# The back half of a decoder layer rebuilt: full-sequence merge, output projection by token chunk, mix and u2 in SBUF, one weight ring for the feed-forward part

## The chip, the cores and the metric

The kernel runs on the 8 cores of one Trainium2 chip. Each core computes one sequence of the batch by itself; the cores do not talk to each other. The time of a run is the device time of the slowest core in microseconds (us). A core has TensorE (PE, the matmuls), VectorE (DVE), ScalarE (ACT), GpSimd (POOL) and SyncE (SP); the last three can also issue DMAs.

## The reference, cut to what matters

```python
# x: (8, 2048, 2048) float32, one decoder layer
u    = rms_norm(x, norm_mix_pre)
proj = u @ w_in                      # q,k,v of 2 x 8 heads of 128, forget logits, g_sb, g_fx
o_sb, o_fx = stick_breaking(...), forgetting_attention(...)        # each (2048, 1024)
merged = sigmoid(g_sb) * (o_sb @ w_branch_sb) + sigmoid(g_fx) * (o_fx @ w_branch_fox)
mix  = merged @ w_out
h    = x + rms_norm(mix, norm_mix_post)
u2   = rms_norm(h, norm_ffn_pre)
ff   = (silu(u2 @ w_gate) * (u2 @ w_up)) @ w_down                  # inner width 5632
out  = h + rms_norm(ff, norm_ffn_post)
```

## The kernel before, in words

Everything is held transposed: model width on the 128 partitions in KC = 16 blocks, tokens along the free axis. A matmul is 128x128 weights by 128x512 tokens; NCH = 4 chunks of 512 tokens make the sequence of 2048, FC = 44 blocks the feed-forward width. The order on each engine is the order in which the program is written out; `kb.op`, `kb.group` and `kb.dma` put semaphore waits in front of an instruction for the last writer and the readers of each buffer (`Res`), and an engine or DMA queue runs its list strictly in that order. `Filler.tick` hands out items of side work while a main loop is written.

The front half (first norm, 16 attention heads with the projections as filler, and the gates `gts`, which go to DRAM as do the head outputs `OTs`) ends with the last piece of the last head: its weights are transposed by DMA into `WTB`, PE multiplies them with V (`pv`), DVE copies the result and SP stores it.

The back half works on halves of 1024 tokens (`TH`), `hf` = 0 and 1:

- `P5(hf)` (merge): one 4 MB load of the head outputs (`OTh`), then for each of 16 blocks the branch weights `wb` (POOL queue), the gates `gb` (SP queue), 2 x 16 matmuls, two DVE products and a POOL sum into `merged`.
- `WOUT(hf)`: output projection, weights `wst` loaded in f32 and cast by DVE; ACT copies each result to `mixst`, stores it to DRAM (`mixs`) and squares it; PE adds up the squares with a matmul by ones (`stat_mm`) and `rstd_from_banks` makes 1/rms.
- `hpass_items`: loads x and `mixs` again, h = x + norm(mix), stored to DRAM (`hs`) by the POOL queue, squared, summed. For half 0 it is filler in `WOUT(1)`, for half 1 in `GATEUP(0)`.
- `u2_items`: loads `hs` again and writes u2. For half 0 it stands alone between `WOUT(1)` and `GATEUP(0)`, for half 1 it is filler in `DOWN(0)`.
- `GATEUP(hf)`: 44 blocks, two weight tiles of 512 KB each (three buffer pairs `wgu`), 64 matmuls; ACT takes silu, DVE the product into `aT`.
- `DOWN(hf)`: 16 blocks, one weight tile `wd` of 1408 KB (three buffers), 2 x 44 matmuls; results go to DRAM (`ffs`), squares to `stat_mm`. `DOWN(1)` runs all 16 blocks for its first 512 tokens and then all again for the other 512, so it loads every `wd` twice.
- `final_items`: loads `hs` and `ffs`, out = h + norm(ff). For half 0 filler in `GATEUP(1)`, then inside `DOWN(1)` and behind it.

`al.release` gives the SBUF of one stage to the next, so the first weights of a stage wait until the buffers that lay there are done with.

## Time and profile before

| | |
|---|---|
| median of 3 runs | 4203.94 us (4196.98 to 4696.29) |
| profiled execution | 4189.77 us |
| its span on the slowest core (core 4) | 4188.2 us |
| spans of the 8 cores | 4130.2 to 4188.2 us |
| DMA, whole span | 553.39 MB, HBM read 617.09 MB, written 109.05 MB |

The span is from the first to the last instruction of a core. Windows of the trace are given in us from the span's start. PEclk is TensorE's granted clock as a share of full speed. A matmul record is longer than the distance to the next one, since matmuls overlap; the rate is read from the busy time of a stretch divided by its matmuls.

### The profile page before, as it was taken

Reading aid. Unit: us, or ns where it says so; the run is one execution under the profiler, and the core shown is the slowest. Engines: PE = TensorE matmul, PEld = TensorE weight load, DVE = VectorE, ACT = ScalarE, POOL = GpSimd, SP = SyncE. Lnnn points to the kernel's source line nnn. Section 1 sums busy time; section 2 is a strip of 40 time slices with the busy share of each in tenths; the row PEclk is TensorE's granted clock in tenths of the full one; section 3 lists DMA queues with packets and bytes.
Section 4 is the critical chain, followed back from the end, with each engine's and each line's share of the span. In section 5 each row is a group of like instructions: output and inputs, shape, how many; then the busy total and the mean of one; then the engine's idle time right before and its main releaser. Section 6 shows DMA issues by size and latency. Waiting matters only on the chain.

```text
span 4188.2 us, 52026 instructions; the slowest of 8 cores (4130.2 to 4188.2 us)
## 1 busy us (share of the span) xinstructions
PE 3764.6 (90%) x17500; PEld 1699.2 (41%) x17500; DVE 1191.8 (28%) x1501; ACT 1046.4 (25%) x1673; POOL 737.3 (18%) x1046
## 2 busy tenths in 40 slices
PE   5999999999999969977639999989999999999973
PEld 2444444444444424433214444434444444444431
DVE  3444445656566523122131111111001111110001
ACT  3456554444444410301211111111110000001100
POOL 0111112222222213033321111110001111110113
PEclk8999999999999989989869999999999999999987
DMA  7212235666665668598885655548537666659997
GB/s 198 44 35 49 50 57 113 119 111 117 116 121 102 136 162 226 172 227 213 226 216 106 123 114 119 115 94 164 126 71 130 115 125 113 126 98 169 184 180 206
DMA packets 358390, 553.39 MB, mean 132 GB/s; under 512 B 200048, under 2 KB 208624, under 8 KB 347888
## 3 DMA queue, kind: packets, MB, share of 16 engines
q0 software_dynamic: 58768, 253.82, 33.4%
q1 hardware_dynamic: 280928, 262.68, 26.7%
q10 hardware_dynamic: 18432, 33.56, 2.5%
q8 instruction: 145, 2.38, 0.2%
q14 instruction: 117, 0.96, 0.1%
HBM read 617.09 MB, written 109.05 MB: 173 GB/s over the span
## 4 chain that ended last, share of the span: by engine, by line
PE 78%; DMA 15%; DVE 2%; issue 2%; POOL 2%; ACT 1%; SPq 0%; DVEq 0%; ACTq 0%; POOLq 0%
PE ps L83 78%; DMA fl_185_227<-ffs 3%; DMA hs<-hst_109_151 3%; DMA xs_21_63<-xT 1%; DMA wd_175_217<-wfd_t 1%; POOL hst_109_151 L83 1%; DMA WTA_95<-wp_62_104 1%; DVE uT_48 L83 1%; DMA mh_107_149<-mixs 1%; DMA hl_133_175<-hs 1%; DMA OTh_136<-OTs 1%; DMA OTh_115<-OTs 1%; DMA WTA_95<-wp_61_103 1%; DMA wd_177_219<-wfd_t 0%; DMA mh_106_148<-mixs 0%
## 5 line engine op out<-in xcount | busy, mean ns | idle before, releaser
L83 DVE TENSOR_TENSOR_SCAN Pr_59_101<-kap_55_97 128x640 f32<-128x640 f32 (+4 forms) x96 | 160.1, 1667 | 124.1 <-POOL kap_55_97 L83 123.3
L83 PE MATMUL ps<-u_124_166,wgu_0_143_185 128*128 128x512 bf16 x480 | 111.1, 385 | 56.3 <-DVE u_124_166 L83 56.3
L83 PE MATMUL ps<-uT_48,wgt_64_106 128*128 128x512 bf16 x704 | 160.5, 379 | 0.0
L83 PE MATMUL ps<-uT_48,wgt_65_107 128*128 128x512 bf16 x704 | 160.0, 379 | 0.0
L83 PE MATMUL ps<-uT_48,wbf_1_8_50 128*128 128x512 bf16 x512 | 128.1, 399 | 34.0 <-DVE uT_48 L83 23.1
L83 PE MATMUL ps<-uT_48,wgt_66_108 128*128 128x512 bf16 x640 | 145.6, 379 | 0.0
L83 PE MATMUL ps<-aT_167,wd_175_217 128*128 128x512 bf16 x484 | 116.3, 404 | 19.9 <-DMA wd_175_217<-wfd_t 19.9
L83 DVE TENSOR_TENSOR_SCAN Pr_60_102<-kap_56_98,Pr_60_102 128x512 f32<-128x512 f32 (+3 forms) x64 | 116.3, 1818 | 48.3 <-ACT kap_56_98 L83 43.6
L83 PE MATMUL ps<-aT_167,wd_153_195 128*128 128x512 bf16 x528 | 117.0, 382 | 13.3 <-DMA wd_153_195<-wfd_t 13.3
L83 POOL TENSOR_SCALAR_AFFINE_SELECT kap_55_97<-kap_55_97 128x128 f32<-128x128 f32 x96 | 40.0, 416 | 485.5 <-ACT kap_55_97 L83 485.1
L83 PE MATMUL ps<-uT_48,wbf_0_7_49 128*128 128x512 bf16 x512 | 121.4, 385 | 0.0
L83 PE MATMUL ps<-uT_48,wbf_1_11_53 128*128 128x512 bf16 x512 | 121.3, 383 | 0.0
L83 PE MATMUL ps<-uT_48,wbf_2_12_54 128*128 128x512 bf16 x512 | 119.6, 379 | 0.0
L83 PE MATMUL ps<-uT_48,wbf_2_9_51 128*128 128x512 bf16 x512 | 119.3, 379 | 0.0
L83 PE MATMUL ps<-uT_48,wbf_0_10_52 128*128 128x512 bf16 x512 | 119.0, 379 | 0.0
L83 PE MATMUL ps<-u_124_166,wgu_0_167_209 128*128 128x512 bf16 x480 | 109.9, 382 | 9.9 <-DMA wgu_0_167_209<-wfg_t 9.9
L83 PE MATMUL ps<-aT_167,wd_176_218 128*128 128x512 bf16 x484 | 107.7, 382 | 6.8 <-DMA wd_176_218<-wfd_t 6.8
L83 PE MATMUL ps<-aT_167,wd_177_219 128*128 128x512 bf16 x440 | 100.9, 391 | 12.8 <-DMA wd_177_219<-wfd_t 12.7
L83 PE MATMUL ps<-u_124_166,wgu_1_170_212 128*128 128x512 bf16 x480 | 108.5, 379 | 0.0
L83 PE MATMUL ps<-u_124_166,wgu_1_168_210 128*128 128x512 bf16 x480 | 108.5, 379 | 0.0
L83 PE MATMUL ps<-u_124_166,wgu_0_169_211 128*128 128x512 bf16 x480 | 108.5, 379 | 0.0
L83 PE MATMUL ps<-u_124_166,wgu_1_144_186 128*128 128x512 bf16 x480 | 108.5, 379 | 0.0
(429 smaller groups left out, 6253.0 us busy)
## 6 DMA issues: line engine op xcount, KB each, us to landing
wd_175_217<-wfd_t POOLq DMA_DIRECT2D x11, 1408.0 KB, 19.0
wd_176_218<-wfd_t POOLq DMA_DIRECT2D x11, 1408.0 KB, 18.5
wd_177_219<-wfd_t POOLq DMA_DIRECT2D x10, 1408.0 KB, 19.8
gts<-gst_67_109 SPq DMA_DIRECT2D x43, 256.0 KB, 2.7
gts<-gst_68_110 SPq DMA_DIRECT2D x43, 256.0 KB, 2.8
gts<-gst_69_111 SPq DMA_DIRECT2D x42, 256.0 KB, 2.9
wd_153_195<-wfd_t POOLq DMA_DIRECT2D x6, 1408.0 KB, 11.6
xs_21_63<-xT SPq DMA_DIRECT2D x8, 1024.0 KB, 16.5
```

The costliest lines, as they stand in the source:

```text
L83: ins = getattr(eng, meth)(**kw)
```

## The change

The front half keeps its instructions; a few buffers move, `OTs`, `gts`, `hs` and `ffs` get a layout in which one load is one contiguous piece of DRAM, and `mixs` is gone. In the back half:

- Merge: all four token chunks of a block follow each other, so each `wb` tile is loaded once. `hook0` to `hook3` start its first loads inside the last head, and merge groups are written between the end of the last head and its last `pv`. DVE makes the sum too.
- Output projection by token chunk, with all 16 weight tiles `wo` in SBUF. `mix` stays in SBUF (20 tiles); `h_item` makes h for the chunk before, stores it, squares it and writes h times the gain over the merge result `M` in bf16. The factor 1/rms of u2 is left out there and is multiplied in `GATEUP` (`rstd2`), in two more DVE instructions for each block and chunk.
- `ring`: the 8 tiles `wo0` to `wo7` become one ring for all feed-forward weights in their order of use; `wd` comes in three pieces of 16, 16 and 12 blocks. A step's tiles are refilled when the step is done.
- The order of `DOWN(1)`: 11 blocks run for both chunks, 5 (9 to 13) for the first chunk only, in between; these 5 follow at the end for the second chunk. Results stay in SBUF (`ff`). `final1` finishes the first chunk during the last 5 blocks and loads `hs` of the second chunk into the buffers it has just stored from.

Names: SP in a DMA row is the queue that issues it; `OT_70`, `OT_71`, `OT_83`, `OT_84` are the head outputs of token chunks 0 to 3, `G_..` the gates, `hm_..` and `ff_0_..` in the last rows are `hl1` and `ff[c][0]`.

PE at the end of the last head, before (`kT`, `qT` scores and `wgt` gates are the last head's, `WTB` its `pv`, `OTh` the merge):

```order
L83 MATMUL ps<-kT_35_77,qT_34_76 128x512 x2
L83 MATMUL ps<-uT_48,wgt_65_107 128x512 x24
L83 MATMUL ps<-WTB_96,V_36_78 128x512 x13
L83 MATMUL ps<-WTB_96,V_36_78 128x384
L83 MATMUL ps<-WTB_96,V_36_78 128x256
L83 MATMUL ps<-WTB_96,V_36_78 128x128
L83 MATMUL ps<-OTh_115,wb_74_116 128x512 x32
```

The same place in the changed kernel:

```order
L83 MATMUL ps<-uT_48,wgt_65_107 128x512 x24
L83 MATMUL ps<-OT_70_112,wb_72_114 128x512 x16
L83 MATMUL ps<-OT_71_113,wb_72_114 128x512 x16
L83 MATMUL ps<-OT_70_112,wb_75_117 128x512 x16
L83 MATMUL ps<-WTB_96,V_36_78 128x512 x13
L83 MATMUL ps<-WTB_96,V_36_78 128x384
L83 MATMUL ps<-WTB_96,V_36_78 128x256
L83 MATMUL ps<-WTB_96,V_36_78 128x128
L83 MATMUL ps<-OT_71_113,wb_75_117 128x512 x16
L83 MATMUL ps<-OT_83_125,wb_72_114 128x512 x16
L83 MATMUL ps<-OT_83_125,wb_75_117 128x512 x16
L83 MATMUL ps<-OT_84_126,wb_72_114 128x512 x16
```

Three merge groups now stand ahead of the last `pv`, and one between it and the first group that reads chunk 2.

SP at the same place before, with the semaphores that each issue waits for (`d_..` are DMAs, `d_Ost1` the store one row above; `e_dve` and so on are engines):

```order
L83 DMA_TRANSPOSE WTB_96<-wp_63_105 128x8x128 [waits e_dve_3]
L83 DMA OTs<-Ost_17_59 128x512 [waits e_dve_3]
L83 DMA OTh_115<-OTs 128x16x1024 [waits d_Ost0_17,d_Ost1_18,e_pe_1,d_v0_0_20,d_v0_1_21,d_v0_2_22,d_v0_3_23,d_v1_0_33,d_v1_1_34,d_v1_2_35,d_v1_3_36]
L83 DMA gb_77_119<-gts 128x1024 [waits e_act_2,e_pool_4]
L83 DMA gb_77_119<-gts 128x1024
```

SP at this place in the changed kernel:

```order
L83 DMA_TRANSPOSE WTB_96<-wp_63_105 128x8x128 [waits e_dve_3]
L83 DMA G_73_115<-gts 128x1024 [waits e_dve_3]
L83 DMA G_74_116<-gts 128x1024 [waits d_gst1_44,e_dve_3]
L83 DMA G_77_119<-gts 128x1024 [waits e_dve_3]
L83 DMA OTs<-Ost_19_61 128x512 [waits e_dve_3]
L83 DMA OT_83_125<-OTs 128x8192 [waits d_Ost0_21,e_pool_4,e_act_2]
L83 DMA OT_84_126<-OTs 128x8192 [waits d_Ost1_22,d_wp0_37,d_wp1_38,d_wp2_39,e_pe_1,d_wgt0_40,d_xs1_0_27,d_xs1_1_28,d_xs1_2_29,d_xs1_3_30]
L83 DMA G_78_120<-gts 128x1024 [waits d_gst2_45,e_dve_3]
```

The one load of a half has become loads of single chunks: those of chunks 2 and 3 stand behind the last store of the head, those of chunks 0 and 1 have moved into the head.

SP in the last blocks, before:

```order
L83 DMA hl_0_189_231<-hs 128x512 [waits d_hl2_0_122,e_pool_4]
L83 DMA fl_192_234<-ffs 128x512 [waits d_ffst0_114,d_fl0_125,e_dve_3]
L83 DMA hl_1_190_232<-hs 128x512 [waits d_hl2_1_123,e_pool_4]
L83 DMA fl_193_235<-ffs 128x512 [waits d_ffst1_115,d_fl1_126,e_dve_3]
L83 DMA hl_2_191_233<-hs 128x512 [waits d_hl2_2_124,e_pool_4]
```

SP in the last blocks of the changed kernel (`d_ff0_0` is the store of `ff_0_204`, two rows above the wait, `d_ff9_0` that of `ff_0_222`):

```order
L83 DMA outT<-ff_0_204_246 128x512 [waits e_dve_3]
L83 DMA hm_236_278<-hs 128x512 [waits d_hb0_76,d_hm0_123]
L83 DMA ff_0_204_246<-hs 128x512 [waits d_hb0_76,d_ff0_0_91]
L83 DMA outT<-ff_0_222_264 128x512 [waits e_dve_3]
L83 DMA hm_237_279<-hs 128x512 [waits d_hm1_124]
L83 DMA ff_0_222_264<-hs 128x512 [waits d_hb1_77,d_ff9_0_109]
```

The stores have moved from the POOL queue into this one, and each load into an `ff` buffer waits for the store two rows above it; there are 16 such triples, and behind them the 16 stores of the second chunk.

The core of the diff:

```diff
+    def hook0():
...
+        ot_load(0)
+        wb_load(0)
+        g_load()
+        g_load()
+
+    def hook1():
+        ot_load(1)
...
+    def hook3():
+        ot_load(2)
+        ot_load(3)
+
+    def m_group():
...
+        for j in range(2):
+            bt, br_ = banks[pr_[j]]
+            kb.op(DVE, "tensor_tensor", dict(out=g.t[:, j, :], in0=bt[:, :], in1=g.t[:, j, :], op=ALU.mult),
+                  writes=[br_], part=[g.r])
+        kb.op(DVE, "tensor_tensor", dict(out=M[tc].t[:, c, :], in0=g.t[:, 0, :], in1=g.t[:, 1, :], op=ALU.add),
+              reads=[g.r], part=[M[tc].r])
+        g_load()
...
+    while mcnt["g"] < len(m_order):
+        m_group()
+        if mcnt["g"] % 8 == 0 and mcnt["g"] >= 24:
+            wo_load(nwo)
+            nwo += 1
...
+    def h_item(tc, c):
...
+        kb.op(DVE, "scalar_tensor_tensor", dict(out=h_.t[:, :], in0=mx.t[:, :], scalar=gcol(1, c),
+                                                in1=rm.t[:, :], op0=ALU.mult, op1=ALU.mult),
+              reads=[mx.r, gains.r, rm.r], writes=[h_.r])
+        kb.op(DVE, "tensor_tensor", dict(out=h_.t[:, :], in0=h_.t[:, :], in1=x_.t[:, :], op=ALU.add),
+              reads=[x_.r], writes=[h_.r])
+        x_fetch()
+        kb.dma(SP, h_.ds, hs[c, tc], h_.t[:, :], reads=[h_.r], writes=[h_res[c][tc]])
+        kb.op(ACT, "activation", dict(out=q_.t[:, :], in_=h_.t[:, :], func=AF.Square), reads=[h_.r], writes=[q_.r])
+        kb.op(DVE, "tensor_scalar", dict(out=M[tc].t[:, c, :], in0=h_.t[:, :], scalar1=gcol(2, c), scalar2=None,
+                                         op0=ALU.mult), reads=[h_.r, gains.r], part=[M[tc].r])
...
+    def ring_fill():
+        while rc_["i"] < min(len(rq), rc_["u"] + 8):
+            src, nf = rq[rc_["i"]]
+            sl = ring[rc_["i"] % 8]
+            kb.dma(POOL, sl.ds, sl.t[:, 0:nf, :], src, writes=[sl.r])
+            rc_["i"] += 1
...
+                kb.op(DVE, "tensor_tensor", dict(out=tb.t[:, :], in0=bg[:, :], in1=r2.t[:, :], op=ALU.mult),
+                      reads=[r2.r], writes=[rg, tb.r])
+                kb.op(ACT, "activation", dict(out=tb.t[:, :], in_=tb.t[:, :], func=AF.Silu), writes=[tb.r])
+                kb.op(DVE, "tensor_tensor", dict(out=tb.t[:, :], in0=tb.t[:, :], in1=r2.t[:, :], op=ALU.mult),
+                      reads=[r2.r], writes=[tb.r])
+                kb.op(DVE, "tensor_tensor", dict(out=aT[f].t[:, t, :], in0=bu[:, :], in1=tb.t[:, :], op=ALU.mult),
+                      reads=[tb.r], writes=[ru], part=[aTr[t]])
...
+    def final1(k):
+        c = fin_order[0][k]
+        final_mul(c, 0)
+        final_add(c, 0)
+        if k + 4 < KC:
+            h_fetch1(fin_order[0][k + 4], 0)
+        c1 = fin_order[1][k]
+        hl_ = ff[c][0]
+        kb.dma(SP, hl_.ds, hl_.t[:, :], hs[c1, 3], reads=[h_res[c1][3]], writes=[hl_.r])
+        h1[(c1, 1)] = hl_
```

## Rows read from the trace of the kernel before

**Rows 1.** The page, part 1: busy us, share of the span, instructions

```profile
PE 3764.6 (90%) x17500; PEld 1699.2 (41%) x17500; DVE 1191.8 (28%) x1501; ACT 1046.4 (25%) x1673; POOL 737.3 (18%) x1046
```

**Rows 2.** Windows of core 4: length, busy per engine, PEclk, DMA share, GB/s

```profile
1533.00:1656.00 123.00, 113.42 (x512) 50.04 (x512) 42.72 (x65) 0.00 (x0) 47.05 (x45) 0.97 0.88 206
...
1776.00:1803.00 27.00, 1.24 (x4) 0.43 (x5) 1.31 (x2) 4.61 (x7) 1.62 (x3) 0.57 0.96 250
1803.00:1917.00 114.00, 112.12 (x511) 50.23 (x509) 43.07 (x64) 0.00 (x0) 46.55 (x45) 0.98 0.87 203
1917.00:2145.00 228.00, 149.01 (x576) 60.55 (x576) 45.15 (x52) 60.90 (x104) 70.94 (x66) 0.86 0.86 229
2145.00:2194.00 49.00, 0.00 (x0) 0.00 (x0) 24.05 (x32) 0.20 (x1) 2.64 (x5) 0.50 0.85 196
2194.00:2812.00 618.00, 617.47 (x2848) 279.20 (x2848) 81.78 (x120) 73.79 (x121) 102.09 (x146) 1.00 0.56 112
2812.00:2825.00 13.00, 0.17 (x1) 0.14 (x2) 2.98 (x5) 3.80 (x5) 1.60 (x3) 0.57 0.87 144
...
3137.00:3149.00 12.00, 0.52 (x2) 0.23 (x3) 1.35 (x2) 3.39 (x6) 3.17 (x6) 0.69 0.85 155
3149.00:3764.00 615.00, 609.20 (x2816) 275.64 (x2814) 81.95 (x120) 53.82 (x89) 103.66 (x149) 1.00 0.63 117
3764.00:3935.00 171.00, 163.00 (x725) 71.97 (x726) 0.69 (x1) 19.11 (x33) 8.44 (x16) 0.96 0.99 171
3935.00:4133.00 198.00, 165.98 (x716) 71.70 (x714) 13.65 (x18) 22.90 (x37) 36.68 (x45) 0.93 0.94 192
4133.00:4189.00 56.00, 0.00 (x0) 0.00 (x0) 12.36 (x16) 0.00 (x0) 29.42 (x32) 0.50 0.70 197
```

**Rows 3.** Timeline at the end of the last head: start, us, what, idle before

```profile
1485.05 5.34 PE L83 MATMUL ps<-uT_48,wgt_65_107 128*128 128x512 bf16 x24
...
1499.08 5.25 PE L83 MATMUL ps<-WTB_96,V_36_78 128*128 128x512 bf16 x16 [8.68 <-DMA WTB_96<-wp_63_105]
...
1506.90 0.37 SPq L83 DMA_DIRECT2D OTh_115<-OTs  x1
1507.42 14.22 SPq L83 DMA_DIRECT2D gb_77_119<-gts  x2
```

**Rows 4.** DMA issues: count, KB each, median us from issue to landing

```profile
gts<-gst_67_109 SPq DMA_DIRECT2D x43, 256.0 KB, 2.7
...
OTh_115<-OTs SPq DMA_DIRECT2D x1, 4096.0 KB, 25.8
...
gb_98_140<-gts SPq DMA_DIRECT2D x16, 512.0 KB, 7.5
...
wgu_0_167_209<-wfg_t POOLq DMA_DIRECT2D x15, 512.0 KB, 8.3
...
fl_164_206<-ffs SPq DMA_DIRECT2D x16, 256.0 KB, 6.2
...
ffs<-ffst_178_220 ACTq DMA_DIRECT2D x16, 256.0 KB, 13.9
...
outT<-ot_195_237 POOLq DMA_DIRECT2D x6, 256.0 KB, 6.2
```

**Rows 5.** Instructions by shape: count, busy us, mean ns, idle before

```profile
L83 DVE TENSOR_TENSOR aT_167<-ps,sg_149_191 128x512 bf16<-128x512 f32 x44 | 30.4, 692 | 264.0 <-PE ps L83 252.8 <-issue 11.2
...
L83 DVE SCALAR_TENSOR_TENSOR hst_138_180<-mh_136_178,gains_45,rstdm_113 128x512 f32<-128x512 f32 x16 | 11.9, 743 | 0.0
...
L83 ACT ACTIVATE mixst_88_130<-ps 128x512 f32<-128x512 f32 x16 | 9.6, 597 | 199.0 <-PE ps L83 199.0
```

**Rows 6.** Timeline behind the last matmul

```profile
4129.73 0.38 PE L83 MATMUL ps<-sqf_181_223,cbf_43 128*128 128x512 bf16 x1 [1.72 <-ACT sqf_181_223 L83]
...
4132.46 0.75 DVE L83 SCALAR_TENSOR_TENSOR ot_195_237<-fl_192_234,gains_45,rstd_126_168 128x512 f32<-128x512 f32 x1 [1.55 <-ACT rstd_126_168 L83]
```

More of the change, by code:

```diff
@@ L369, in _emit @@
     make_qkv(0)
+    Ost = [Slot(kb, f"Ost{i}", [128, 512], BF16, dma=True) for i in range(2)]
     m_q1 = al.mark()
@@ new lines, in evict0, with fin_ready, first @@
+    def evict0(c, t, bt, br_):
+        fs = ffst[evn["n"] % 4]
+        evn["n"] += 1
+        kb.op(ACT, "activation", dict(out=fs.t[:, :], in_=bt[:, :], func=AF.Copy), writes=[br_, fs.r])
+        kb.dma(SP, fs.ds, ffs[c, t], fs.t[:, :], reads=[fs.r], writes=[ff_res[c][t]])
+    evn = {"n": 0}
+    def fin_ready(hf, t):
+        if hf == 0:
+            if t == 1:
+                def first():
+                    for _ in range(3):
+                        f_fetch()
+                hq.append(first)
+                hq.extend([lambda n=n: final0(n) for n in range(2 * KC)])
+        else:
+            hq.extend([lambda k=k: final1(k) for k in range(KC)] if t == 0 else [])
```

723 lines of the change are left out of this document (362 added, 361 removed).

## The prediction, made before the changed kernel had run

> **What bounds the kernel now.** I read the page first: PE is busy for 3764.6 of 4188.2 us, with 17,500 matmuls [rows 1]. The order of both programs has the same 17,498 matmuls, so the change can only take away time in which PE stands, and the question is where it stands. The windows by stage answer that [rows 2]. In 2194 to 2812 PE does 2848 matmuls in 617.47 us at a granted clock of 1.00, the upper level of 2.4 GHz: 0.2168 us each, with no gap. I take that as the price of a matmul. The last gate matmuls end at 1485.05 + 5.34 = 1490.4 [rows 3]; from there to the end lie 2697.8 us. In them stand the last pv (16 matmuls, 3.5 us) and 10,688 more: merge 1024, output projection 1024, gate and up 5632, down 2816, sums of squares 192. They are worth 2317.2 us. So PE stands for 377 us behind 1490.4, and the change touches no time ahead of that.
>
> The windows say where: 39 us from the last gate matmul to the first merge matmul at 1533 (42.6 less pv), 12 in the rest of the first merge (123 less 512 matmuls), 26 at the second merge's start, 103 in the second output projection with its h pass (228 less 576 matmuls), 49 while u2 is made alone, 13 and 12 at the borders of the feed-forward stages, 5 in the second gate and up, 57 in the last down stage (369 less 1441 matmuls), 55 behind the last matmul [rows 2, 3]. That is 371 of the 377.
>
> **The change part by part.**
>
> *End of the last head.* PE stood 8.7 us for the last transposes, and pv then ran for 5.25 us, cold, where 3.5 is the price [rows 3]. Three merge groups (10.4 us) now fill that gap; they need chunks 0 and 1, asked for some tens of us earlier. Then one group (3.5 us) covers what follows pv: copy (0.7 us), store, load of chunk 2. The 4096 KB load took 25.8 us [rows 4]; half of it is 12.9. Issued 1.4 us behind pv it lands at 14.3, so PE waits 10.8; two groups follow (6.9, and 1.8 for the lower clock after a gap, as pv showed), and chunk 3 lands some 4 us after them. I take 16 us; from 3 (rows of 16 KB run much faster than the 2 KB pieces before) to 25 (both loads and the gates share the DMA engines). The Trainium skill (DMA: Bandwidth & Descriptors, Anatomy of one DMA) gives 2 us and bytes over 436 GB/s for a DMA of GpSimd's queue; for 4096 KB that would be an estimated 11.6 us, and the trace's 25.8 us on SP's queue disagrees; by it a chunk would land in 6.8 us, this term would be about 5, and the time 11 us less.
>
> SP's loads inside the head stand ahead of its transposes. A 4096 KB load held up SP's next issues for 14.22 us [rows 3], so two of 2048 KB may hold it for 7 each. pv comes long behind the transposes and the three `wp` buffers give some slack; I take 3 us, 0 to 10.
>
> *Merge.* Four groups (13.9 us) ask for one `wb` and four gate tiles of 512 KB; before it was two and four, and 1803 to 1917 was 112.12 of 114 us busy at a DMA share of 0.87 [rows 2]. The gates are asked for four groups ahead, 11 us net of DVE, and landed in 7.5 [rows 4]. DVE has three products of 0.69 us [rows 5] in each 3.5. Nothing is added; the 12 and 26 us are gone.
>
> *Output projection.* Six of 16 weight tiles are loaded in the merge, ten at its end. A tile costs the 16 DMA engines at most 618 x 0.56 / 88 = 3.9 us [rows 2], with all else that ran then, so the last lands 39 + 8 us later and is used at 15 x 3.7 = 55. A block and chunk takes 18 matmuls, 3.9 us; ACT has a copy and two squares, 3 x 0.60 = 1.8, DVE three operations, at most 2.2 [rows 5]. The h pass no longer waits for `mixs` and `hs` to land, it reads SBUF, and its x loads and h stores have three buffers, 11 us. So the 103 us go. The 49 us of u2 go too: chunks 0 and 1 have been written long before gate and up starts.
>
> *Gate and up.* Per block and chunk (32 matmuls, 6.94 us) DVE has three products and for some steps three operations of side work, at most 2.1 + 2.2 us, and ACT one silu. The chain behind the gate matmuls is about 3.5 us, and PE has three bank pairs. One weight tile is used per 6.94 us, six are under way (41 us) and they land in 8.3 [rows 4]. Nothing on the path. In the second half, though, the final items now go one per step for 33 steps, 768 KB in 6.94 us. Behind the last matmul 48 such transfers of 256 KB took 56 us at a share of 0.70 [rows 2], 0.82 us each of the whole DMA; with the weights that makes 2.5 + 3.9 = 6.4 of 6.94. It fits, barely. I take 5 us, as now; 0 to 100.
>
> *Borders.* The ring loads the next stage's tiles while the last blocks run: 13 and 12 us go. What hides them is PE's own work: a stage begins with eight tiles loaded.
>
> *Last down stage.* Weights come 21 times instead of 32. Under a DMA share of 0.99 and 0.94 a load of 1408 KB took 369 / 32 = 11.5 us [rows 2]. The 16 first steps (11 of 19.1 us, 5 of 9.5) leave room. The last five take 9.5 us each; the ring holds 2.7 steps ahead, so 3.3 x 11.5 = 38 us of loads have to land in 38. They just do, alone; but the first chunk's stores and the `hs` loads go on beside them, some 22 of 0.82 us. I take 12 us of waiting, 0 to 25, for the 57 now.
>
> *Behind the last matmul.* Here lies a new wait. SP takes 16 triples: store, load, load into the buffer just stored, and the third waits for the first to land, with all later stores and loads queued behind it. A store of 256 KB landed in 2.7 us beside attention, 6.2 at the end, 13.9 under full DMA [rows 4]; with two issues a link is 3.7 us when quiet, and I take 7.8 beside the last weights. The chain starts when the first chunk's sum is known, five steps (47 + 12 us) before PE ends: 7 links are done then, 9 x 3.7 = 33 us remain, then 16 stores of the second chunk, 16 x 0.82 = 13, and 4 to land the last. Tail 50 us, against 55 now. Low: the chain keeps up, 2.7 us to 1/rms [rows 6], 16 x (0.74 + 0.69) = 23 on DVE, 6.2 to land: 32. High: links of 14.7 first, then 7: 100.
>
> *Sum.* 1490.4 + 3.5 + 2317.2 = 3811.1. Waits 16 + 3 + 5 + 12 = 36. Tail 50. Span 3897; the profiled execution lies 1.6 us above its span, 3899, and the median of the runs shown 14.2 above the profiled execution: **3913 us**, 291 less, a ratio of 0.931.
>
> **The rivals.**
>
> *The end drags.* The chain of stores runs at 14.7 us beside the weights and 7 behind them, and the last five steps wait 25: 3913 + 50 + 13 = 3976. For it: stores landed in 13.9 us in this very stage, and everything at the end is on SP. Against: the writes of `ffs` are gone and a third of the weights.
>
> *Nothing is left.* The 16, 12 and 18 of the tail go to their low ends: 3913 - 13 - 12 - 18 = 3870.
>
> *Side work crowds the second gate and up.* DVE is in order, so a final item that waits for its load holds back the products and PE's banks. 33 steps at 3 us more: 4012. For it: 6.4 of 6.94. Against: loads are asked for two steps ahead, 13.9 us, and landed in 6.2 [rows 4].
>
> *The resident weights are not resident in time.* If the ten late tiles land one after the other at 8.3 us each [rows 4], the last comes at 83, 28 us late: 3941. It needs that no two loads overlap; six did in gate and up.
>
> *Slower: the ring starves.* All feed-forward weights now pass one ring and one queue in strict order. Should a tile arrive less often than once in 6.94 us, PE runs at the tiles' pace, 176 times. The gain is used up at 6.94 + 291 / 176 = 8.6 us per tile; at 10 us the time is 3913 + 176 x 3.06 = 4452. For it: a single load already lands in 8.3 us, and DVE, GpSimd and DMA all get denser here. Against: even in the saturated last stage 1408 KB took 11.5 us, 4.2 per 512 KB, half of what would be needed.
>
> **How the numbers follow.** The forecast's own case has 0.72, the dragging end 0.12, nothing left 0.05, crowding 0.05, late resident weights 0.03, the starving ring 0.03. The range from 3870 to 3990 takes in the first three and the late weights, with the bounds of the tail, of the last steps and of chunk 2 and 3; crowding and starving stay out. About 2% is what a measurement here can tell from no change, 4120 to 4288. All cases but the last lie below it: faster 0.95, same 0.02, slower 0.03.
>
> **What would show it right or wrong.** Right: matmuls of merge chunk 0 ahead of the last pv; one gap of 10 to 15 us behind it; no gap from there to the last five blocks; a matmul at 0.217 us through all of gate and up; the chain of waits ending in stores of `ff` on SP's queue with links of 4 to 8 us. Wrong: PE waiting for `wo` tiles inside the stages (the ring), for DVE in the second gate and up (crowding), for ACT in the output projection, or a last head that takes longer than before. The forecast would also fail if PE's denser work were granted less than 1.00 of its clock, which no row here shows.

## The result, and the profile after

The changed kernel took 3917.8 us in the median of four runs (3914.6 to 3945.4), the kernel before 4203.9 beside it (4197.0 to 4217.9): a ratio of 0.932, 95% interval 0.927 to 0.938. Executions in which a die was granted a lower clock, and one of 4696.3 us of the kernel before, are left out of all times here and below. Forecast were 3913 us and 0.931. The time was right; some terms of the sum were not, and their errors cancelled. Below it is told which.

Busy times of the changed kernel, page, part 1. PE has the same 17,500 matmuls as in [rows 1], 11.5 us less busy, in a span 244 us shorter; DVE has 318 us more.

```profile
PE 3753.1 (95%) x17500; PEld 1700.1 (43%) x17500; DVE 1509.4 (38%) x2013; ACT 1053.0 (27%) x1675; POOL 443.9 (11%) x789
```

The profiled execution is the longest of the four, and for a reason ahead of the change: core 4 was granted 0.91 of its clock from 900 to 1200 and did 1279 matmuls there; before it was 1.00 and 1389. So I measure from a reference point, the last head's scores of 256 columns (the matmul that waits 1.20 us for `bet_58`), at 1373.45 on core 4 before and at 1400.68 after. From it to the end the sum of the forecast has 3897 - 1373.4 = 2523.6 us. The changed kernel took 2524.7, 2525.8 and 2520.9 on cores 0 to 2, 2543.2 on core 4, and 2521 to 2551 on all eight, 2535 in their mean.

Windows of core 0 (columns as in [rows 2], to which they answer): end of the last head, merge, output projection, gate and up, down, gate and up, down, behind the last matmul. They are cut at the first matmul of each stage but for one: 2014.95 lies behind the last sum of squares of the output projection, and gate and up had begun at 2011.09. The table below is cut there.

```profile
1376.66:1512.84 136.18, 119.23 (x544) 54.32 (x556) 64.44 (x60) 49.70 (x75) 26.62 (x40) 0.95 0.72 167
1512.84:1750.17 237.33, 225.76 (x1021) 102.13 (x1040) 132.80 (x191) 2.54 (x3) 15.33 (x29) 0.99 0.80 212
1750.17:2014.95 264.78, 253.76 (x1130) 113.79 (x1154) 98.53 (x155) 110.94 (x189) 4.24 (x8) 0.98 0.43 122
2014.95:2622.55 607.60, 604.60 (x2760) 275.44 (x2816) 212.55 (x313) 71.81 (x111) 45.90 (x87) 1.00 0.48 87
2622.55:2933.15 310.60, 309.13 (x1413) 140.84 (x1440) 0.69 (x1) 37.02 (x62) 24.38 (x46) 1.00 0.49 100
2933.15:3542.70 609.55, 605.16 (x2762) 275.63 (x2818) 226.51 (x329) 61.55 (x96) 47.49 (x90) 1.00 0.59 119
3542.70:3855.12 312.42, 309.58 (x1412) 140.77 (x1439) 16.31 (x25) 40.64 (x67) 29.71 (x56) 1.00 0.55 108
3855.12:3901.40 46.28, 0.00 (x0) 0.00 (x0) 27.76 (x44) 1.26 (x2) 0.00 (x0) 0.51 0.66 226
```

Read the PEld counts, since matmul records are missing on this core: 1440 weight loads in a down stage of 310.60 us, 0.2157 us each, at a clock of 1.00 and without a gap. Side by side with the sum of the forecast, stage by stage:

| from the reference point, us | forecast | core 0 | other cores |
|---|---|---|---|
| end of the last head | 117 + 3 = 120 | 136.2 | 130.4 to 144.2 |
| merge with the last `pv` | 3.5 + 222 + 16 = 241.5 | 237.3 | 234.8 to 241.8 |
| output projection | 246.3 | 260.9 | 258.6 to 269.9 |
| gate and up, first | 614.0 | 611.5 | 611.5 |
| down, first | 312.2 | 310.6 | 310.6 |
| gate and up, second | 610.5 + 5 = 615.5 | 609.6 | 609.5 |
| down, second | 312.2 + 12 = 324.2 | 312.4 | 312.4 to 312.8 |
| behind the last matmul | 50 | 46.3 | 46.8 to 59.4 |
| sum | 2523.7 | 2524.7 | 2520.9 to 2550.6 |

Three readings follow from it. The feed-forward part, 1844 us, has no gap but 1.3 us ahead of its last matmul. The last head, whose instructions the change leaves alone but for loads put into it, got 13 to 27 us longer. And the end of the kernel is as long as before.

**The last head.** PE at that place, core 4 (timeline; [rows 3] answers to it). The first three rows are waits that the kernel before did not have; then the three merge groups ahead of `pv`, `pv` itself without a wait (8.68 us before), one group behind it and one gap (the last row shows 12 of its 16 matmuls).

```profile
1444.38 7.34 PE L83 MATMUL ps<-uT_48,wgt_66_108 128*128 128x512 bf16 x24 [11.79 <-ACT gst_69_111 L83]
...
1478.27 5.30 PE L83 MATMUL ps<-uT_48,wgt_65_107 128*128 128x512 bf16 x16 [4.48 <-ACT gst_67_109 L83]
1487.27 0.80 PE L83 MATMUL ps<-kT_35_77,qT_34_76 128*128 128x512 bf16 x2 [3.70 <-ACT bet_58_100 L83]
...
1551.12 3.62 PE L83 MATMUL ps<-OT_70_112,wb_75_117 128*128 128x512 bf16 x16
1554.57 3.30 PE L83 MATMUL ps<-WTB_96,V_36_78 128*128 128x512 bf16 x16
1557.71 3.62 PE L83 MATMUL ps<-OT_71_113,wb_75_117 128*128 128x512 bf16 x16
1570.28 4.94 PE L83 MATMUL ps<-OT_83_125,wb_72_114 128*128 128x512 bf16 x12 [8.96 <-DMA OT_83_125<-OTs]
```

The first wait is for `gst_69`, a buffer that ACT fills with gates and SP stores. SP's queue shows why it was not free (timeline of core 4, SP alone): the load of chunk 0, two gate tiles, then the gate store, so behind 3 MB of loads. Behind the store comes a transpose whose issue alone takes 10.65 us, and the store of the third buffer, `gst_68`, has to wait for that.

```profile
1424.45 0.32 SPq L83 DMA_DIRECT2D OT_70_112<-OTs  x1
1424.94 0.33 SPq L83 DMA_DIRECT2D G_73_115<-gts  x1
1425.36 0.38 SPq L83 DMA_DIRECT2D G_74_116<-gts  x1
1425.84 1.73 SPq L83 DMA_DIRECT2D gts<-gst_69_111  x1
1427.66 0.42 SPq L83 DMA_DIRECT2D gts<-gst_67_109  x1
1428.17 10.65 SPq L83 DMA_TRANSPOSE WTB_96<-wp_63_105  x1
1438.92 0.52 SPq L83 DMA_DIRECT2D gts<-gst_68_110  x1
```

The chain of waits has the other end (start, us, what): that store landed 17.71 us after its issue, where such stores took 2.7 before [rows 4]; then ACT evicts into the buffer, and PE goes on.

```profile
1425.84 17.71 DMA gts<-gst_69_111
...
1443.63 0.61 ACT gst_69_111 L83
```

The DMA issues of the last 105 us of the head (issue to landing, us) say that the loads themselves are quick: a chunk of 2048 KB landed in 11.8 and 9.9 us, where 4096 KB took 25.8 [rows 4].

```profile
OT_70_112<-OTs SPq DMA_DIRECT2D x1, 2048.0 KB, 11.8
OT_71_113<-OTs SPq DMA_DIRECT2D x1, 2048.0 KB, 9.9
```

**The end.** Timeline of core 4 from the last matmul on ([rows 6] answers to it). PE is done at 3892.7. The 1/rms of the second chunk needs only its bank, but its first step, the `TENSOR_SCALAR` into `tmpD`, stands 24.7 us later, behind the additions of the first chunk on DVE.

```profile
3892.35 0.38 PE L83 MATMUL ps<-sqf_185_227,cbf_43 128*128 128x512 bf16 x1 [1.31 <-ACT sqf_185_227 L83]
...
3916.81 0.69 DVE L83 TENSOR_TENSOR ff_0_234_276<-ff_0_234_276,hm_239_281 128x512 f32<-128x512 f32 x1 [3.82 <-DMA hm_239_281<-hs]
3917.42 0.68 DVE L83 TENSOR_SCALAR tmpD_229<-ps 128x512 f32<-128x512 f32 x1
```

Those additions wait for loads which SP issues in its chain. Four links of it, from the chain of waits of core 4: 11.87 and 12.06 us beside the last weights, then 3.55, and 3.19 to 3.36 from there on.

```profile
3855.93 11.87 DMA outT<-ff_0_222_264
...
3868.28 12.06 DMA outT<-ff_0_206_248
...
3880.82 3.55 DMA outT<-ff_0_208_250
...
3884.86 3.19 DMA outT<-ff_0_224_266
```

### The profile page after: what moved, and what is told of

The parts are those of the page before. It is cut to its first block, busy times and chain, and to the rows that moved or that the text cites. A ratio compares the mean times of both kernels' runs of the same rounds, so it can differ in the third digit from the quotient of the medians.

```text
span 3943.9 us, 50744 instructions; the slowest of 8 cores (3879.0 to 3943.9 us)
## 1 busy us (share of the span) xinstructions
PE 3753.1 (95%) x17500; PEld 1700.1 (43%) x17500; DVE 1509.4 (38%) x2013; ACT 1053.0 (27%) x1675; POOL 443.9 (11%) x789
## 4 chain that ended last, share of the span: by engine, by line
PE 88%; DMA 6%; DVE 2%; ACT 2%; issue 1%; SPq 0%; POOL 0%; DVEq 0%; ACTq 0%; POOLq 0%
PE ps L83 88%; DMA xs_20_62<-xT 1%; DMA WTA_95<-wp_62_104 1%; DMA G_77_119<-gts 1%; DVE uT_48 L83 1%; DMA gts<-gst_69_111 0%; DMA gts<-gst_68_110 0%; DMA WTA_95<-wp_61_103 0%; SPq L83 0%; DMA outT<-ff_0_206_248 0%; ACT kap_56_98 L83 0%; DMA outT<-ff_0_222_264 0%; ACT bet_58_100 L83 0%; DMA OT_83_125<-OTs 0%; DMA hs<-hb_126_168 0%
## 5 line engine op out<-in xcount | busy, mean ns | idle before, releaser
L83 PE MATMUL ps<-uT_48,wgt_65_107 128*128 128x512 bf16 x704 | 168.8, 394 | 4.5 <-ACT gst_67_109 L83 4.5
L83 PE MATMUL ps<-uT_48,wgt_64_106 128*128 128x512 bf16 x704 | 166.7, 389 | 0.0
L83 PE MATMUL ps<-uT_48,wgt_66_108 128*128 128x512 bf16 x640 | 152.4, 392 | 11.8 <-ACT gst_69_111 L83 11.8
L83 PE MATMUL ps<-uT_48,wbf_1_8_50 128*128 128x512 bf16 x512 | 130.4, 405 | 32.7 <-DVE uT_48 L83 23.1
L83 ACT ACTIVATE tg_139_181<-tg_139_181 128x512 f32<-128x512 f32 x60 | 37.8, 630 | 338.6 <-DVE tg_139_181 L83 338.6
L83 ACT ACTIVATE tg_141_183<-tg_141_183 128x512 f32<-128x512 f32 x58 | 36.5, 630 | 334.1 <-DVE tg_141_183 L83 334.1
L83 ACT ACTIVATE tg_140_182<-tg_140_182 128x512 f32<-128x512 f32 x58 | 36.5, 629 | 330.8 <-DVE tg_140_182 L83 330.8
L83 PE MATMUL ps<-uT_48,wbf_0_7_49 128*128 128x512 bf16 x512 | 122.8, 388 | 0.0
L83 PE MATMUL ps<-uT_48,wbf_1_11_53 128*128 128x512 bf16 x512 | 122.8, 386 | 0.0
L83 PE MATMUL ps<-uT_48,wbf_2_12_54 128*128 128x512 bf16 x512 | 121.5, 383 | 0.0
L83 PE MATMUL ps<-uT_48,wbf_2_9_51 128*128 128x512 bf16 x512 | 121.0, 383 | 0.0
L83 PE MATMUL ps<-uT_48,wbf_0_10_52 128*128 128x512 bf16 x512 | 120.5, 383 | 0.0
L83 PEld LDWEIGHTS ps<-uT_48,wgt_65_107 128*128 128x128 bf16 x704 | 70.8, 101 | 92.4 <-issue 22.8
L83 PEld LDWEIGHTS ps<-uT_48,wgt_64_106 128*128 128x128 bf16 x704 | 69.8, 100 | 84.7 <-issue 19.1
L83 PEld LDWEIGHTS ps<-uT_48,wgt_66_108 128*128 128x128 bf16 x640 | 63.9, 100 | 90.5 <-issue 29.5
L83 POOL TENSOR_SCALAR_AFFINE_SELECT bet_57_99<-bet_57_99 128x128 f32<-128x128 f32 x96 | 95.7, 997 | 57.9 <-ACT bet_57_99 L83 57.7
L83 POOL TENSOR_SCALAR_AFFINE_SELECT kap_55_97<-kap_55_97 128x128 f32<-128x128 f32 x96 | 39.3, 409 | 518.0 <-ACT kap_55_97 L83 517.7
L83 PEld LDWEIGHTS ps<-uT_48,wbf_1_8_50 128*128 128x128 bf16 x512 | 52.1, 103 | 98.9 <-issue 53.3
L83 ACT ACTIVATE bet_57_99<-ps 128x640 f32<-128x640 f32 (+4 forms) x96 | 74.4, 775 | 19.3 <-ACT kap_55_97 L83 15.1
```

Source lines behind the costliest of these rows:

```text
L83: ins = getattr(eng, meth)(**kw)
```

## The experiments

They ran on other chips, where the kernel before took 4146 to 4190 us. One of them, told below, is by its order the changed kernel again: 3919.4 us, 3908.2 in the mean of its cores' spans; the changed kernel's own runs had means of 3902 to 3909. So I compare times and stage lengths with these, not ratios. "Head" is the first row of the table above; in kernels that leave it alone it was 129 to 148 us, 136 to 140 in the mean of the eight cores. Lengths of the output projection are cut as in the table.

### The last head: queue order or full DMA engines

Theory A: the loads hold up SP's queue, and the gate stores and transposes behind them make PE wait. Rival B: the DMA engines are full, whichever queue is used. Four edits.

*Loads on ScalarE's queue.*

```diff
-        ot_load(0)
...
-        g_load()
-        g_load()
+        steps.after(4.0, lambda: (ot_load(0, ACT), g_load(ACT), g_load(ACT)))
...
-        ot_load(1)
+        steps.after(4.0, lambda: ot_load(1, ACT))
```

> The loads of chunks 0 and 1 and of the first two gate tiles, asked for inside the last head, go out on ScalarE's DMA queue instead of SyncE's, about 4 us of program later; the bytes are the same. Measure: from the last sigmoid ahead of the first merge load (bet_58 near 1400) to the end of the last gate matmul, 131 to 144 us by core in the changed kernel, 117 before. Theory A (the gate stores and the transposes stand in SyncE's queue behind 3 MB of loads, so the three gate buffers are not free and TensorE's gate matmuls wait for ScalarE): the waits of 10 to 12 us for a gate buffer go, the stretch falls to 117 to 122, the time by 12 to 20 us, to about 3902. Rival B (the 16 DMA engines are full, whichever queue asked): the gate stores land just as late, the stretch stays at 130 to 144, the time within 5 us of 3918.

Measured: head 127.4 to 137.4 on cores 0 to 3, mean 131.5, a gain of about 5 (the other four were granted a lower clock); time 3915 to 3916. SP's queue on core 1 has neither chunk 0 nor its gate tiles in it any more, and yet (timeline, SP and ACT; the load went out at 1398.53):

```profile
1398.71 0.54 SPq L83 DMA_DIRECT2D gts<-gst  x1
...
1401.78 10.53 SPq L83 DMA_TRANSPOSE WTB<-wp  x1
...
1412.42 1.24 SPq L83 DMA_DIRECT2D gts<-gst  x2
...
1416.60 0.60 ACT L83 ACTIVATE gst<-ps 128x512 f32<-128x512 f32 x1 [10.28 <-DMA gts<-gst]
```

The issue of a transpose took 10.53 us with the load on another queue (this load landed in 14.1 us), so the hold-up of a transpose does not need a load on its own queue. ACT, which has the sigmoids of attention behind the gate, stood 10.28 us. What ended that is the landing of the store in the first row, which had gone out ahead of the transpose (chain of waits of core 1):

```profile
1398.71 17.81 DMA gts<-gst
```

It took as long as in the changed kernel (17.71), though no load stood in its queue. From 1398 to 1413 the 16 DMA engines of this core were busy all the time: 51.5% of it with ScalarE's queue, 44.8% with GpSimd's, which loads weights, and 3.1% with SP's. So on the stores rival B is right here: they land just as late. But the head is some 5 us shorter, where B expected no gain, and A more than twice that.

*Gate stores on ScalarE's queue*, loads as they were:

```diff
-    kb.dma(SP, st_.ds, gts[n % KC, tc, :, n // KC, :], ...
+    kb.dma(ACT, st_.ds, gts[n % KC, tc, :, n // KC, :], ...
```

> The gate stores of the whole kernel go out on ScalarE's DMA queue instead of SyncE's; all loads stay where the changed kernel has them. Measure: from the last head's 256-wide score matmul to the first merge matmul, 130 to 144 us by core in the changed kernel (mean 138), 117 at that point before. Theory A (order on SyncE: what stands behind the loads waits): the waits for a gate buffer, 10 to 12 us, go; the transposes stay behind the loads, so 3 to 10 us come back as waits for the attention weights; stretch 122 to 132. Rival B (the DMA engines are full): a gate store lands just as late on a queue of its own, the waits for a gate buffer stay within 3 us of what they were, stretch 130 to 144.

Head 125.8 to 132.6 on cores 0 to 5, mean 129.0 (cores 6 and 7, at a granted clock of 0.87 and 0.86 there, took 142 and 143); times 3911.5 and 3930.3. PE's waits on core 1 in that stretch: none for a gate buffer, one for the transposes of `pv`.

```profile
PE ps L83 <- DMA WTB<-wp: 7.1, 1, 7.1
PE ps L83 <- ACT bet L83: 1.4, 1, 1.4
```

The stretch and the waits are about those of theory A. But a store with a queue of its own is not free of the loads: the slowest took 10.1 to 13.8 us to land on these six cores, where it was 15.4 to 17.7 in the changed kernel and a store took 2.7 before [rows 4]. So in these runs the busy engines delay the stores on either queue, and what stands ahead in the queue adds to it.

*The load in pieces of 512 KB*, some 6 us of program apart:

```diff
-        ot_load(0)
+        for p in range(4):
+            steps.after(1.0 + 6 * p, lambda p=p: ot_piece(0, p))
```

> The loads of chunks 0 and 1 inside the last head are cut into four pieces of 512 KB each, asked for some 6 us apart on the same queue; the first branch weights and the first two gate tiles follow them. Same bytes. Theory C (a single load of 2048 KB keeps all 16 DMA engines for its 10 us, so that a transpose issued behind it, on whichever queue the load is, is held up as long, and the gate stores behind the transpose with it): no hold-up is longer than 3 us, the three gate buffers and the three weight buffers cover that, the stretch falls from 138 to 117 to 122 and the mean span of the cores from 3904 by 14 us or more. Rival B (too many bytes for the stretch): the waits only spread out, stretch 130 or more, span within 6 us.

Head 123.4, 124.1, 126.8 and 134.9 on cores 0 to 3, mean 127.3: ten better, not the 17 to 20 that theory C wanted; times 3906.3, 3910.7 and 3930.3, mean spans of 3897 to 3909. The long waits are gone (at most 4 to 6 us remain), and what stays is open; the stretch carries 7.5 MB of chunks, gate tiles and branch weights that it did not carry before.

*All loads asked for later*, with the third chunk's output:

```diff
-        attn_sb(..., hooks=(hook0, hook1, hook2, hook3) if fin else ())
+        attn_sb(..., hooks=(nohook, nohook, hook012, hook3) if fin else ())
```

> The same four loads stay on SyncE's queue but are asked for only with the third chunk's head output, some 45 us before the head ends, together with the next two gate tiles. Theory A (order in the queue) and rival B (full DMA engines) agree that the two stalls inside the head at 1425 to 1445 and 1465 to 1487 go, about 15 us; they differ behind it: 6 MB now stand in one piece in the queue. By A the stores and transposes of the head's last 45 us are held for some 25 us and one stall of 10 to 20 us comes back there, so the time stays within 8 us of 3918. By B (bytes only, 6 MB over 45 us is no more than the DMA did around 1425) little comes back and the time falls by 10 us or more.

Head 135.0 to 139.1: on cores 0 to 3 the two waits became one of 17.4 to 19.5 us for a gate buffer. Time 3915 to 3917. That is what A expected, and the hold-up moves with the loads; by the runs above it does not tell order from full engines.

### The end: the chain of stores

```diff
-        c1 = fin_order[1][k]
-        hl_ = ff[c][0]
+        for j in ([k - LAG] if k >= LAG else []) + (list(range(KC - LAG, KC)) if k == KC - 1 else []):
+            c1 = fin_order[1][j]
+            hl_ = ff[fin_order[0][j]][0]      # LAG = 4
```

> The load of the second chunk's h into a buffer just stored from is asked for four triples later, so that it finds its store landed; instructions and bytes are the same. Theory A (each of the 16 links waits for a store to land, 3.6 us when quiet and 8 to 12 beside the last weights; VectorE is in order, so the second chunk's 1/rms waits behind the last link): the links end before the last matmul, the tail behind the last matmul falls from 51 to about 31 us (2 for the sum, 2.7 for 1/rms, 16 products and sums at 1.27, 6 for the last store), the time by 15 to 22 us, to about 3899. Rival B (the DMA engines' throughput sets the pace: 768 KB per triple beside the weights): triples still come 2.5 to 3.4 us apart, the tail falls by less than 8 us.

Behind the last matmul 27.5 to 32.7 us remain instead of 46 to 59, as theory A had it; 1/rms starts 3.2 us after the last matmul on core 0 (3877.80, last matmul done at 3874.63). But the mean span fell by 15 only, to 3888 to 3891, and the time to 3905.3. The rest went into a new wait: the last down stage grew to 313.7 to 320.6 us, because PE waits for weights where it had not. With SP no longer slowed by its own waits, its transfers now go out beside the last weights (core 0, 319.0 us instead of 312.4):

```profile
PE ps L83 <- DMA wo<-wfd_t: 4.4, 2, 2.8
PE ps L83 <- ACT sqf L83: 1.3, 1, 1.3
```

### The output projection: what its 103 us had been

Mix through DRAM again, asked for early:

```diff
+            kb.dma(ACT, mx.ds, mixs[c, tc], mx.t[:, :], reads=[mx.r], writes=[mix_res[c][tc]])
+            mixq.append(lambda ...: kb.dma(SP, mx.ds, mx.t[:, :], mixs[c, tc], ...))
+            if len(mixq) > 4:
+                mixq.pop(0)()
```

> Every output projection result is also stored to DRAM and loaded back into the same SBUF tile four steps later, before the h pass reads it 12 steps after that: 64 stores and 64 loads of 256 KB more. Theory A (of the 103 us that the second output projection and its h pass stood, the trip of mix through DRAM was the cause): the output projection of the changed kernel, 266 us, grows by 30 us or more. Theory B (the cause was the chain of one h item, load, VectorE, GpSimd, store, with two buffers, in which a trip asked for early does not count): it grows by less than 8 us, since a step of 3.7 to 3.9 us has room for four transfers at 0.82 us.

The output projection took 274 to 285 us, 278 in the mean of the cores, about 10 more than the 266 to 269 of other kernels on these chips; time 3927. Between the two, nearer to B: 32 MB more at a DMA share of 0.78 cost 10 us.

One buffer for x and one for h:

```diff
-        x_, h_, q_, mx = xb[n % 3], hb[n % 3], sqh[n % 2], mix[n % 20]
+        x_, h_, q_, mx = xb[0], hb[0], sqh[n % 2], mix[n % 20]
```

> One buffer instead of three for the x loads and one instead of three for the h tiles of the h pass. Theory A (the output projection before stood for its h items: each held one of two buffers while its loads and its store were under way): a cycle of one buffer is 0.74 + 0.69 us of VectorE, 4.1 until the store has landed and about 0.5 between, 6.0 us for a step of 3.7 to 3.9, in some 49 steps: the output projection grows from 265 to 272 us to about 380. Rival B (what it stood for was the bytes, DMA share 0.86): with the same bytes it grows by less than 20 us.

347.7 to 354.6 us, about 85 more; 4007.7 us in all (one run). PE's waits in the output projection of core 0:

```profile
PE ps L83 <- ACT sqh L83: 81.4, 41, 7.1
PE ps L83 <- DVE G L83: 4.8, 1, 4.8
```

The same bytes, and nearly the old loss back: theory A. My 110 were too many, because with one item at a time a store landed in 3.2 us, not 4.1. This shows what a chain of few buffers can cost; it does not rebuild the old one, in which an item had two buffers and its store landed only after 8 us, behind GpSimd's part. What DVE waited for there (the kernel before, core 4, 1917 to 2145; the two largest):

```profile
DVE hst_109_151 L83 <- DMA hs<-hst_109_151: 76.2, 11, 9.7
DVE hst_108_150 L83 <- DMA mh_106_148<-mixs: 43.3, 8, 10.3
```

With the other buffer of each kind it is 96 us for stores of h to land and 53 for loads of `mixs`: the buffers held the old chain longest, and the trip through DRAM had its share, asked for late as it was.

### The last down stage: bytes of weights or of `ffs`

```diff
-            one = [13, 12, 11, 10, 9]
+            one = list(range(15, -1, -1))
```

> The last down stage in the order of the kernel before: all 16 blocks for the first 512 tokens, then all 16 again for the others, so that it loads 32 times 1408 KB instead of 21. Theory A (loads bounded this stage before): 1408 KB cost the DMA 9.0 us (615 us at a share of 0.47 for 88 tiles of 512 KB), 32 of them and 48 transfers of 0.8 us for the first chunk's end make 327 us or more against 305 us of matmuls: the stage grows from 312 to 335 to 365 us. The first chunk is done 150 us ahead, so its chain of stores is over and the tail behind the last matmul falls from 51 to about 30. Time 3905 to 3935. Rival B (the stage was held by its order and its stores, not by the weights): the stage stays within 5 us of 312, and with the shorter tail the time falls to about 3895.

The stage took 321.1 to 323.7 us, not 335 to 365; behind the last matmul 25.5; times 3899.0, 3899.6 and 3924.7. Loading every weight twice costs 10 us, not 57. My price of 9.0 us per block was wrong: at a DMA share of 0.91 over 323 us, less 48 transfers at 0.8, a block's 1408 KB cost an estimated (294 - 38) / 32 = 8.0 us, under the 9.5 that PE works on it.

The same with `ffs` too:

```diff
+        kb.dma(ACT, f_.ds, ffs[c, 2 + t], f_.t[:, :], reads=[f_.r], writes=[ff_res[c][2 + t]])
...
+    def ff_back(c):
+        kb.dma(SP, ff[c][0].ds, ff[c][0].t[:, :], ffs[c, 2], reads=[ff_res[c][2]], writes=[ff[c][0].r])
```

> The last down stage with 32 weight loads, as in the run that loads twice (stage 321 to 324 us), and besides each result of this stage is stored to DRAM and the first chunk's 16 are loaded back into their tile before its end is made of them: 48 transfers of 256 KB more, as the kernel before had them. Theory A (the 57 us that this stage stood before were bytes: not the second passage of the weights alone, but that and the ffs trips together): 48 x 0.8 = 38 us of DMA more in a stage whose DMA was nearly full; the stage grows to 345 to 365 us. Rival B (it stood because weights were asked for only two steps ahead, and a tile of 1408 KB landed in 19 us; the ring of eight small tiles is what took it away): the stage stays below 332 us.

334.4 to 340.1 us, 339.2 on core 0, time 3928.3 (one run), between the two. On core 0 (waits of PE in this stage, this kernel):

```profile
PE ps L83 <- DMA wo<-wfd_t: 18.5, 10, 3.1
PE ps L83 <- ACT sqf L83: 1.7, 1, 1.7
```

Weights twice and `ffs` together make 22 to 28 of the old 57 us, 27 on core 0. The bytes are then nearly those of the kernel before, 65.75 MB against 67.15. The same stage here and in the kernel before (core 4):

```profile
3543.00:3883.00 340.00, 319.70 (x1444) 141.69 (x1442) 21.17 (x30) 40.64 (x67) 47.27 (x89) 0.98 0.99 193
3764.00:4133.00 369.00, 328.98 (x1440) 143.66 (x1440) 14.34 (x19) 42.01 (x69) 45.12 (x61) 0.94 0.96 182
```

The old stage had its DMA engines busy too, 0.96 of 369 us, which is 354 us where 337 do here: 17 us more for 2% more bytes. Why the same loads and stores took the engines longer, and what made the rest of the 30 us, stays open. Two things differ that were not tried by themselves: the depth, two blocks asked for ahead instead of eight smaller tiles, and the layout, tiles of 1408 KB and `hs` and `ffs` not in contiguous pieces.

### The borders, and asking for the merge's loads late

A first edit stopped the ring at the borders in the program text:

```diff
-        while rc_["i"] < min(len(rq), rc_["u"] + 8):
+        end = min(b for b in (88, 136, 224, len(rq)) if b > rc_["u"] or b == len(rq))
+        while rc_["i"] < min(end, rc_["u"] + 8):
```

> The weight ring stops at each border of the feed-forward stages: the first eight tiles of a stage are asked for only when the last step of the stage before is done. Theory A (the borders stood 13 and 12 us before because the first weights of a stage were asked for too late, and crossing the border is what takes that away): at three borders PE waits for tiles that land in 5 to 9 us each, eight of them asked for together; 8 to 14 us per border, 25 to 40 us in all, in the first steps of the stages behind them. Rival B (a border also needs the last products of the stage before, and the gap went with the shorter eviction): 5 us or less per border, under 15 in all.

Nothing: stages of 611.5, 310.6, 609.6 and 312.4 us, 3919.4 in all. The edit was void. GpSimd has nothing else to issue between two stages, so its order and its waits are the same in both programs. The run serves as the repetition named above. The second edit makes the first load of a stage wait for the last matmuls of the stage before, and also asks for the merge's first loads only behind the last head's gates:

```diff
+            if rc_["i"] in (88, 136, 224):
+                for s in ring:
+                    for ev in kb._deps([], [s.r]):
+                        POOL.wait(ev)
...
         filler.flush()
+    hook0()
+    hook1()
+    hook2()
```

> Two undone parts at places that do not touch each other. (1) At each border of the feed-forward stages the ring now really waits: its first load of the next stage waits until the last matmul of the stage before has read its tile, seven tiles follow it at once. Theory A (crossing the border is what took the 13 and 12 us away): PE waits at three borders for tiles, 6 to 9 us where gate and up begins (one tile to land), 10 to 14 where a down stage begins (three tiles), 26 to 37 in all. Rival B: 5 us or less each. (2) The first loads of the merge are asked for behind the last head's gate matmuls instead of inside the head. Theory A (the loads hold up the head by 18 us, but save the merge a wait): the head's stretch to its last gate matmul falls to 117 to 120 and the first merge matmul waits 20 to 30 us for its chunk, the gate tiles and the weights, so the merge starts 138 to 150 us after the reference point, 0 to 12 later than in the changed kernel. Rival B: the loads land in 12 us or less and the merge starts at 130 or earlier, so that asking early cost more than it gave.

3968.6 us. PE's waits on core 0 from the reference point on:

```profile
PE ps L83 <- DMA OT<-OTs: 35.8, 3, 23.5
PE ps L83 <- DMA wo<-wfd_t: 30.1, 3, 15.5
...
PE ps L83 <- DMA wo<-wfg_t: 7.5, 1, 7.5
```

Theory A in both parts, in one run. The borders cost 7.5 us at gate and up and 30.1 at the two down stages, 37.6 together (28.6 to 33 on cores 1 to 3), up to 15.5 at one border where 10 to 14 were expected. And without loads inside it the head ran 117 us to its last gate matmul, as before the change; the first merge matmul then waited 21 to 23.5 us, so that the merge began 137.6 to 140.2 us after the reference point, at the same point as in the changed kernel, and took 244 to 248 us instead of 235 to 242. Of the wait that asking early hides, the hold-ups in the head give all back; what it gains are some 7 us in the merge.

### A version from the findings

The load in pieces, the gate stores on ScalarE's queue, the late load two triples later, and three more edits:

```diff
-    m_order[0:8] = [(0, 0), (0, 1), (1, 0), (1, 1), (0, 2), (1, 2), (0, 3), (1, 3)]
+    m_order[0:12] = [(c, tc) for c in range(3) for tc in range(2)] + [(c, tc) for c in range(3) for tc in (2, 3)]
...
-        if mcnt["g"] % 8 == 0 and mcnt["g"] >= 24:
+        if mcnt["g"] % 4 == 0 and mcnt["g"] >= 16 and nwo < 12:
...
-            one = [13, 12, 11, 10, 9]
+            one = [15, 14, 13, 12, 11, 10, 9, 8]
```

> A version of its own: chunks 0 and 1 loaded in four pieces each inside the last head; gate stores on ScalarE's queue; two more merge groups on chunks 0 and 1 behind the last pv; the resident weights of the output projection asked for one tile per four merge groups from the sixteenth on; eight instead of five blocks of the last down stage put last for the second chunk; the load into a stored buffer two triples later. By the runs so far: head 138 to about 120 (18), the wait for chunk 2 from 7 to 0, the gates at the merge's end 4 to 0, the tail from 51 to about 28 with 3 to 7 us of waits for weights: 18 + 7 + 4 + 18 = 47 us below a mean span of 3905, so 3858 in the mean and about 3870 for the slowest core. Rival: stores on ScalarE's queue and pieces do the same thing twice (head 125), and the wait for chunk 2 only moves into the gates: 3880 or more for the slowest core.

3881.5 us (3880.9 to 3883.3), against 3919.4 of the one repetition on the same chip: 38 us faster than the changed kernel, a ratio to the kernel before of 0.934, 0.930 to 0.939. The mean of the cores is 3870 to 3875, not 3858. By stage on cores 0, 1, 2 and 4: head 118.7 to 133.9 (mean 127.6, 128.6 on all eight), merge 229 to 231 (7 to 9 less; 4 us of waits for chunks 2 and 3 remain, none for gates), last down stage 321.7 to 322.8 (10 more, 7 to 8 of them waits for weights), behind the last matmul 25.4 to 26.6 (some 25 less). So the rival was right about the head: pieces and stores on another queue do not add up. On core 1 the pieces hold the transposes up one after the other until `pv` has to wait (timeline, SP and then PE):

```profile
1434.82 4.19 SPq L83 DMA_TRANSPOSE WTA<-wp  x1
...
1439.71 5.54 SPq L83 DMA_TRANSPOSE WTA<-wp  x1
...
1448.60 6.23 SPq L83 DMA_TRANSPOSE WTA<-wp  x1
...
1460.95 4.32 PE L83 MATMUL ps<-WTA,V 128*128 128x512 bf16 x10 [12.18 <-DMA WTA<-wp]
```

## Why the prediction was right, and where its steps were off

*The path.* That PE's standing time behind 1490.4 was the whole stake, and that nothing in the feed-forward part would take its place, held: 1844.1 us for its four stages against 1866 forecast. Part of that difference is the price of a matmul: 0.2157 us (310.60 / 1440), not 0.2168, which makes 12 us over 10,688. The stretch from which the price was read has all its 2848 records, but it begins with 16 matmuls that took 6.23 us, where 16 take 3.62 later, at a granted clock of 0.50 from 2194 to 2198, after 56.3 us without work; from 2200 to 2800 it has 2782 in 600.00 us, 0.2157 each.

*End of the last head, SP's loads inside it: 3 us, bounds 0 to 10.* This step failed: 13 to 27. I had named the transposes as what is queued behind the loads and found slack for them in three `wp` buffers. I had not named the gate stores, which stand behind the loads and the transposes on the same queue and have three buffers used every 3.5 us. The run with the stores on another queue took away the wait for them and some 8 us, the run with late loads had the hold-up where the loads went, and without loads in it the head took its old 117. Shown, then: beside the loads the slowest gate store lands in 15.4 to 17.7 us instead of 2.7, and PE waits for its buffer. How much of that is order on SP and how much full DMA engines is not settled: with the loads on another queue a store landed as late, on a queue of its own in 10.1 to 13.8 at the slowest. That the issue of a transpose can take 10 us beside a load on either queue was seen, its cause inside the DMA hardware was not tested.

*Chunks 2 and 3: 16 us.* One gap of 6.6 to 9.0 and none for chunk 3: mis-sized by 7 to 9. Chunk 2 was issued 1.5 us behind `pv`, as forecast, and landed in 8.4 to 10.7 us, not 12.9. By the Trainium skill (DMA: Bandwidth & Descriptors, Anatomy of one DMA), whose fit is for GpSimd's queue, it would be an estimated 6.8; the trace disagrees with both.

*Merge: "nothing is added".* Nearly. Some 45 us ahead of its end eight resident weight tiles are asked for within 4 us, and four more some 10 us ahead of it; a gate tile then landed in 14.7 us on core 0 and 17.7 on core 4, and PE waited 1.7 to 6.2. In the last version, which spreads them, this wait is gone.

*Output projection.* The 103 us went, but 10 to 17 us of waits stay, most of them for `sqh` about the start of a chunk, where h items follow the 1/rms of the chunk before, and the granted clock is 0.97 to 0.99. I had put nothing there. The cause of the old loss, which I gave as "reads SBUF" and "three buffers" in one sentence, is mostly the buffers, as far as the runs go: with one each, 85 us come back, with the trip through DRAM asked for early 10. The old arrangement itself was not rebuilt. That the 49 us of u2 are gone is seen in the windows; no run undid that part.

*Second gate and up: 5 us.* None. The estimate of 6.4 us of DMA in a step of 6.94 was not far off; the share of the stage is 0.59 because the final items last for 33 of 88 steps.

*Borders.* Right, and undone they cost more than they had: 29 to 38 us.

*Last down stage: 12 us, for the 57 before.* None was left. The saving of the 57 was put down to 21 loads in the place of 32; that is a small part of it. Loading all twice costs 10 us, with the `ffs` trips 27, and 30 stay open. The price of 11.5 us for a block's weights, the whole stage divided by 32, held the other transfers and the waits of that stage as well; by the run that loads twice it is an estimated 8.0.

*Behind the last matmul: 50 us.* 46 to 59, and the chain of stores as described, with links of 3.2 to 3.6 on core 4 when quiet (3.7 forecast) and 7.7 to 12 beside the weights (7.8). What the step had not seen is the way in which it reaches the end: not through the last stores, but through DVE, where the second chunk's 1/rms stands behind the first chunk's last addition. Untied, the tail is 28 to 33 us; the low end of the forecast was 32.

*The sum.* By the table, on core 0: too low by 16 in the head and 15 in the output projection; too high by 12 in the last down stage, 10 in the other three feed-forward stages, 4 in the merge and 4 at the end. That this cancels to 1 us is luck, and core 0 is one of the three shortest: in the mean of the eight the sum is 11 too low. Two of the signs that the prediction named for being wrong came, a longer last head and waits for ACT in the output projection, and the gap-free stretch from `pv` to the last blocks did not. Of the rivals none came true; the dragging end has its mechanism, not its price.

## What to carry to other kernels

When a load is moved into another stage, list for each engine's queue everything that stands behind it, the stores with few buffers first, and ask who waits for those buffers: what a prefetch hides can be lost where it is issued. Another queue helps less than it seems, since here all queues shared the same 16 DMA engines: read the landing times too. Do not let a load into a buffer wait for a store just above it in an in-order queue; two to four triples later the wait is free, but then the freed queue crowds its neighbours, so read the stage again. And what a rebuilt stage no longer loses need not be owed to the part that looks largest: undo the parts one by one, and see that the edit really moved something in the order.
